# Turned probabilities of an attention step: one copy of both heads in place of one copy per head

## What is computed

```python
# layer 0 (8 heads): compressed, selected and window attention, gated
o = gc[..., 0:1] * o_cmp + gc[..., 1:2] * o_slc + gc[..., 2:3] * o_win
# layer 1 (16 heads): attention over the keys an indexer picked
o = jnp.einsum('bgrqk,bqkgd->bqgrd', masked_softmax(s, mask), vg)
# layer 3 (16 heads): dilated attention, three patterns folded into one mask
o = dilated_attention(q, k, v)
```

## Time and profile before

| what | value |
|---|---|
| median of three runs | 2514.33 us |
| profiled execution, its own time | 2514.71 us |
| its span, first to last instruction | 2513.0 us |
| mean granted TensorE clock | 0.980 of full speed |
| busy share: TensorE, VectorE, ScalarE, GpSimd | 96%, 53%, 37%, 43% |
| pass 0, pass 1, pass 2 in the span | 188 to 284, 837 to 925, 2021 to 2095 us |

### The profile page before, as it was taken

The page is one execution under the profiler, slowest core; times in us unless marked ns, Lnnn a source line. Parts: engine busy times, 40 slices in busy tenths (PEclk is TensorE's granted clock), DMA queues, the critical chain, the costliest instruction groups (busy, mean ns, idle before and its releaser), DMA issues.

```text
span 2513.0 us, 35279 instructions
## 1 busy us (share of the span) xinstructions
PE 2407.1 (96%) x12149; PEld 1946.9 (77%) x12149; DVE 1334.2 (53%) x2348; ACT 937.8 (37%) x1523; POOL 1085.3 (43%) x513
## 2 busy tenths in 40 slices
PE   7997989999999799999999989999999999999998
PEld 6774678888876467888887768888888967888887
DVE  6778664443157855111127976545366555545445
ACT  3356433222233463322234444322246364432222
POOL 2335334444443343444444734444454454444443
PEclk9999989999999899999999999999999999999999
DMA  7540235554322102323332213323333211232322
GB/s 308 195 149 26 98 132 190 184 184 159 99 94 76 34 34 76 106 95 96 97 100 84 76 51 119 113 87 101 100 101 102 91 34 48 87 109 84 109 92 75
DMA packets 64341, 263.64 MB, mean 105 GB/s; under 512 B 7265, under 2 KB 7777, under 8 KB 57953
## 3 DMA queue, kind: packets, MB, share of 16 engines
q1 hardware_dynamic: 61056, 251.00, 29.9%
q10 hardware_dynamic: 3168, 11.08, 1.2%
HBM read 259.95 MB, written 2.10 MB: 104 GB/s over the span
## 4 chain that ended last, share of the span: by engine, by line
PE 57%; issue 22%; POOL 9%; DVE 5%; ACT 2%; DVEq 2%; POOLq 1%; DMA 1%; SPq 0%; ACTq 0%
PE bank L638 17%; PE bank L640 17%; PE bank L639 17%; POOL w_lo L582 9%; PE bank L823 2%; PE bank L813 1%; DVEq L1761 1%; PE bank L842 1%; DVE acc L1559 1%; ACT prob L1282 1%; POOLq L629 1%; DVE bank L2177 1%; DVE prob L1741 1%; PE bank L760 0%; PE bank L659 0%
## 5 line engine op out<-in xcount | busy, mean ns | idle before, releaser
L582 POOL TENSOR_TENSOR w_lo<-raw,w_hi 128x1024 fp32r<-128x1024 f32 x378 | 918.1, 2437 | 1263.4 <-ACT w_hi L1168 1262.0
L638 PE MATMUL bank<-h_hi,w_hi 128*128 128x512 f32 x1760 | 698.4, 397 | 15.1 <-DVE h_lo L1606 7.8
L639 PE MATMUL bank<-h_lo,w_hi 128*128 128x512 f32 x1760 | 691.0, 393 | 0.0
L640 PE MATMUL bank<-h_hi,w_lo 128*128 128x512 f32 x1760 | 690.8, 393 | 0.0
L1168 ACT ACTIVATE w_hi<-raw 128x1024 fp32r<-128x1024 f32 x378 | 392.6, 1051 | 472.9 <-PE bank L640 469.9
L638 PE MATMUL bank<-g_hi,w_hi 128*128 128x512 f32 x1072 | 418.5, 390 | 0.0
L640 PE MATMUL bank<-g_hi,w_lo 128*128 128x512 f32 x1072 | 417.2, 389 | 0.0
L639 PE MATMUL bank<-g_lo,w_hi 128*128 128x512 f32 x1072 | 417.1, 389 | 0.0
L638 PEld LDWEIGHTS bank<-h_hi,w_hi 128*128 128x128 f32 x1760 | 334.3, 190 | 92.8 <-DVE h_lo L1606 8.7
L640 PEld LDWEIGHTS bank<-h_hi,w_lo 128*128 128x128 f32 x1760 | 334.1, 190 | 71.5
L639 PEld LDWEIGHTS bank<-h_lo,w_hi 128*128 128x128 f32 x1760 | 334.5, 190 | 68.5 <-issue 0.5
(11 more groups left out here) (298 smaller groups left out, 2610.5 us busy)
## 6 DMA issues: line engine op xcount, KB each, us to landing
raw<-in_panels SPq DMA_DIRECT2D x378, 512.0 KB, 3.5
modraw<-in_pairs SPq DMA_DIRECT2D x40, 1024.0 KB, 5.9
first_mods<-in_first SPq DMA_DIRECT2D x4, 2048.0 KB, 22.0
w<-in_w ACTq DMA_DIRECT2D x2, 2048.0 KB, 8.6
x<-in_x SPq DMA_DIRECT2D x1, 2048.0 KB, 8.3
out<-yout ACTq DMA_DIRECT2D x8, 256.0 KB, 2.2
mask<-in_causal ACTq DMA_DIRECT2D x1, 1024.0 KB, 5.7
mask<-in_dilated ACTq DMA_DIRECT2D x1, 1024.0 KB, 7.1
```

The lines of the kernel that those rows point to most:

```text
L582: pool.tensor_tensor(w_lo[:, slot, :], raw[:, slot, :], w_hi[:, slot, :].bitcast(F32), ALU.subtract)\
L638: pe.matmul(out, w_h, m_h, start=start, stop=False)
L639: pe.matmul(out, w_h, m_l, start=False, stop=False)
L640: return pe.matmul(out, w_l, m_h, start=False, stop=stop)
```

## The change

Banks 2 and 3 become one PSUM tensor, and one operation copies the same columns of both banks. ScalarE and VectorE do this by turns of steps. In pass 0 ScalarE has the even (wide) steps and VectorE the odd ones. In pass 1 ScalarE has all of the first 16 steps. In the rest of pass 1 and in pass 2 ScalarE has the steps with n mod 4 of 0 or 3, VectorE those with 1 or 2. `turn(n)` signals once, after both heads, and starts when both heads of step n-1 are copied.

```diff
-        bank = [ctx.enter_context(nc.psum_tensor(f"bank{n}", [P, 512], F32)) for n in range(8)]
+        bank = [None if n in (2, 3) else ctx.enter_context(nc.psum_tensor(f"bank{n}", [P, 512], F32)) for n in range(8)]
+        turned = ctx.enter_context(nc.psum_tensor("turned", [P, 2, 512], F32))
+        bank[2], bank[3] = turned[:, 0, :], turned[:, 1, :]
...
-        def odd_by_scalar(run, n):
-            return run == 0 and n % 2 == 1 or run == 1 and n < N_PAIR // 2 and n % 2 == 0
+        def copied_by_scalar(run, n):
+            return n % 2 == 0 if run == 0 else n % 4 in (0, 3) or run == 1 and n < N_PAIR // 2
...
                 def turn(n):
                     pe.wait_ge(weights_ready, at + n + 1)
-                    for b, copied in enumerate((pt_even, pt_odd)):
-                        if n:
-                            pe.wait_ge(copied, at + n)
+                    if n:
+                        pe.wait_ge(pt_copied, at + n)
+                    for b in range(2):
                         for j in range(pairs_[n][0] + 1):
                             m = pe.transpose(bank[2 + b][:, P * j:P * j + P],
                                              prob[:, PROB_SLOT[n % PROB_STEPS], b, P * j:P * j + P], ident[:, :])
-                        m.then_inc(pt_done, 1)
+                    m.then_inc(pt_done, 1)
...
-                    pe.wait_ge(pt_even, at + n + 1)
-                    pe.wait_ge(pt_odd, at + n + 1)
+                    pe.wait_ge(pt_copied, at + n + 1)
...
-                def copy_even(n):
-                    act.wait_ge(pt_done, 2 * (at + n) + 1)
+                def copy_turned(n):
+                    act.wait_ge(pt_done, at + n + 1)
                     if n >= 2:
                         act.wait_ge(pv_done, at + n - 1)
                     w = P * (pairs_[n][0] + 1)
-                    act.activation(probT[:, 2 * (n % 2), 0:w], bank[2][:, 0:w], ACT.Copy).then_inc(pt_even, 1)
-                    if odd_by_scalar(run, n):
-                        act.wait_ge(pt_done, 2 * (at + n) + 2)
-                        act.activation(probT[:, 2 * (n % 2) + 1, 0:w], bank[3][:, 0:w], ACT.Copy).then_inc(pt_odd, 1)
+                    act.activation(probT[:, 2 * (n % 2):2 * (n % 2) + 2, 0:w], turned[:, :, 0:w], ACT.Copy).then_inc(pt_copied, 1)
...
-                    if n >= SCORES_AHEAD:
-                        copy_even(n - SCORES_AHEAD)
+                    if n >= SCORES_AHEAD and copied_by_scalar(run, n - SCORES_AHEAD):
+                        copy_turned(n - SCORES_AHEAD)
...
-                def copy_odd(n):
-                    dve.wait_ge(pt_done, 2 * (at + n) + 2)
+                def copy_turned(n):
+                    dve.wait_ge(pt_done, at + n + 1)
                     if n >= 2:
                         dve.wait_ge(pv_done, at + n - 1)
                     w = P * (pairs_[n][0] + 1)
-                    dve.tensor_copy(probT[:, 2 * (n % 2) + 1, 0:w], bank[3][:, 0:w]).then_inc(pt_odd, 1)
+                    dve.tensor_copy(probT[:, 2 * (n % 2):2 * (n % 2) + 2, 0:w], turned[:, :, 0:w]).then_inc(pt_copied, 1)
...
-                    if n >= SCORES_AHEAD and not odd_by_scalar(run, n - SCORES_AHEAD):
-                        copy_odd(n - SCORES_AHEAD)
+                    if n >= SCORES_AHEAD and not copied_by_scalar(run, n - SCORES_AHEAD):
+                        copy_turned(n - SCORES_AHEAD)
```

More of the change, by code:

```diff
@@ L320, in build @@
         pt_done = sem("pt_done")
-        pt_even = sem("pt_even")
-        pt_odd = sem("pt_odd")
+        pt_copied = sem("pt_copied")
         pv_done = sem("pv_done")
@@ L1288, in attention @@
                 for n in range(N_PAIR - SCORES_AHEAD, N_PAIR):
-                    copy_even(n)
+                    if copied_by_scalar(run, n):
+                        copy_turned(n)
                     if group_ended(run, n - 1):
@@ L1739, in masked @@
                     if n >= PROB_STEPS:
-                        dve.wait_ge(pt_done, 2 * (at + n - PROB_STEPS) + 2)
+                        dve.wait_ge(pt_done, at + n - PROB_STEPS + 1)
                     dve.tensor_tensor_reduce(row_of(n, b, w), bank[SBANK[(2 * n + b) % 3]][:, 0:w], mask[:, i, 0:w],
@@ L1790, in attention @@
                 for n in range(N_PAIR - SCORES_AHEAD, N_PAIR):
-                    if not odd_by_scalar(run, n):
-                        copy_odd(n)
+                    if not copied_by_scalar(run, n):
+                        copy_turned(n)
                     if group_ended(run, n - 1):
```

## The result

The changed kernel takes 2521.17 us, the median of 6 runs (2519.45 to 2528.27); the kernel before, run beside it, 2514.1 (6 runs, 2512.0 to 2514.89). The ratio is 1.0033, 95% interval 1.002 to 1.0046: slower by 7.1 us. A second measurement of the same two kernels gave 2520.84 (7 runs) against 2513.95 (10 runs), ratio 1.003, 1.0019 to 1.0042. The profiled execution after took 2519.45 with a span of 2517.7; before it was 2514.71 and 2513.0.

A forecast was written before the change was run, and what follows sets the result against it. The prediction took chains of waits through the copy, not full engines, to bound the attention passes. Terms +6.4, +3.1 and -1.4 sum to +8.1 on 2514.71, giving 2522.8, less 0.4 for the median: 2522.4 us, range 2517 to 2526.

The forecast's parts named there:

- the mechanism in pass 2: Pass 2: exps, `out_high`, `out_low` and next masking stand behind the copy; rounds of 4.36 become 4.90 and 4.72 us.
- the end of pass 0: Pass 0, last steps draining one by one, with VectorE copying step 31: +0.45 us.
- Pass 2: Pass 2: even rounds +0.54 or +0.41, odd +0.36 or +0.23, end 1.2; together +6.4 us.
- The price of the copy: Joined copy of 2 x 512 columns, start to next start: 0.90 us on ScalarE, 1.14 on VectorE.
- Pass 1: Pass 1: rounds 9 to 14 and the end as in pass 2, rounds 1 to 8 put at 0; +3.1 us.
- Pass 0: Pass 0: VectorE loses the wide copy, gains the narrow one and reaches the inversion sooner in most rounds; -1.4 us.
- A late pass is passed on in full.: Behind each pass: TensorE begins a projection at once, so the passes' +8.1 us reaches the whole time.
- The wait before `out_low`: Pass 2, VectorE's wait for `out_high`, 0.75 us before: claimed to grow in even rounds.
- The second: Whole kernel: engine time decides, long copies are made up next round; about -4 us, 2510; chance 0.16.
- The third: Copy over two banks costs two single ones: +1.7 us, 2524; chance 0.12 together with the fourth.
- The fourth: Pass 0 gains nothing, ScalarE's wide copy (0.90 us) delaying exps and `out_high`: 2524; chance 0.12 together with the third.
- The rule: Skill's grouping advice: larger operations help saturated engines, smaller pieces where others wait; passes 1 and 2 put under the latter.

The follow-up runs named there:

- e1: Kernel before, with only the change's joined signal and wait, copies still split per head; 2517.5 us (one run).
- e3: Changed kernel; VectorE has every joined copy in pass 1's second half and pass 2, ScalarE the last ones of pass 0; 2522.0 us (one run).
- e2: Changed kernel, with every joined copy on ScalarE; 2512.8 us (one run).
- e7: Changed kernel, with VectorE's copies placed behind the masking of the second head and the inversion; 2523.6 us (one run).
- e8: Changed kernel once more, unedited; 2520.84 us (7 runs).
- e9: Kernel before once more, unedited; 2513.95 us (10 runs).
- e4: Kernel before, with one joined copy per step by ScalarE in all of pass 0; 2505.06 us (8 runs), ratio 0.9966.
- e10: Kernel before, with ScalarE also copying the second head of pass 0's wide steps, in two operations a step; 2500.91 us (4 runs), ratio 0.9944.
- e11: Kernel before, copies split: ScalarE copies both heads in pass 0, VectorE's copies stand behind second-head masking and inversion; 2499.49 us (5 runs), ratio 0.9944.

## Why the prediction came out right, point by point

The direction and the time held (2522.4 forecast, 2521.2 measured), and so did the mechanism in pass 2, which e1 to e3 show. The time held partly by luck: the passes grew by 11.9 us and not by 8.1, and the rest of the program, put at 0, became shorter. Three terms were mis-sized or left out: the end of pass 0, the start of ScalarE's copy in the first half of pass 1, and the clock outside the passes.

- **Pass 2, +6.4 forecast, +6.5 measured** (+6.6 in the second pair). Even rounds +0.53 (0.54 forecast) and +0.44 (0.41); odd +0.36 (0.36) and +0.25 (0.23); the end behind round 15 +1.22 (1.2): the 20 last matmuls of the earlier trace rows begin 8.02 after the start of round 15 (at 2099.09) where it was 6.71. Rounds 0 to 2, put at 0 but for round 2's 0.54, gave 0.53 together. e1 excludes the wait, e2 and e3 show each term alone.
- **The price of the copy.** 1.02 and 1.22 us for 2 x 512, start to next start 0.92 and 1.14, where 0.90 and 1.14 were put. The Trainium skill, "VectorE: DVE Perf Modes", section "The TRN2 errata — SBUF-src ops pay a fixed extra latency per instruction", gives 172 + N cycles at 1.2 GHz for a ScalarE copy out of PSUM and 120 + N at 0.96 for VectorE; for N = 1024 that is an estimate of 1.00 and 1.19 us. The trace agrees within 3%.
- **Pass 1, +3.1 forecast, +3.9 measured** (+4.0 in the second pair). Rounds 9 to 14 and the end gave 2.06 + 1.22, near the forecast 1.9 + 1.2. The first half was put at nothing, since ScalarE's joined copy of a wide step would begin 0.05 later than the first of its two had. That is the step that failed. The first of the two needed one turned head only; the joined one needs both, and begins 0.4 us later. Round 8, first before (it begins at 886.42), then after (885.87):

```profile
887.79 1.09 PE L823 MATMUL bank<-ident,prob 128*128 128x128 f32 x8
...
888.48 0.60 ACT L1256 ACTIVATE probT<-bank 128x512 f32<-128x512 f32 x1
```

```profile
887.24 1.09 PE L824 MATMUL turned<-ident,prob 128*128 128x128 f32 x8
...
888.37 1.02 ACT L1256 ACTIVATE probT<-turned 128x1024 f32<-128x1024 f32 x1 [0.60 <-PE turned L824]
```

Both turns begin 1.37 after the round's start, the copy 0.69 and 1.13 after the turn's, and the round takes 5.14 for 4.77. Rounds 2 and 4 together grew by 0.67 (0.75 in the second pair); in round 4 TensorE turns at the lower clock, 1.97 us for 1.09, and the copy begins 1.15 and 2.01 after the turn's start. Rounds 6 and 7 became 0.2 shorter each. e1, with the joined signal and the copies still split, has at least the same growth (round 8 5.21, rounds 2 and 4 together 15.06 for 14.13), so here it is the signal that costs and not the copy.
- **Pass 0, -1.4 forecast, +1.4 measured** (+0.6 in the second pair, where round 2 of the kernel before was longer). Here is the term that was mis-sized most. The rounds gave -1.44 against -1.85: round 2 -1.41 (-1.35), round 4 -0.27, round 12 -0.36 (-0.35), and round 3 went the other way, +0.32 for -0.27. The end gave +2.8 in place of +0.45, which had left out that the copy of step 29 stands behind VectorE's side work. Its timeline after:

```profile
278.13 0.55 DVE L1845 SCALAR_TENSOR_TENSOR modsum<-modraw,csil,modsum 128x256 f32<-128x256 f32 x1
278.60 0.15 DVE L1755 RECIPROCAL stat<-stat 128x2 f32<-128x2 f32 x1
...
278.93 0.69 DVE L1749 COPY probT<-turned 128x512 f32<-128x512 f32 x1
...
279.76 0.84 PE L824 MATMUL turned<-ident,prob 128*128 128x128 f32 x6 [2.19 <-DVE probT L1749]
...
281.60 1.09 PE L824 MATMUL turned<-ident,prob 128*128 128x128 f32 x4 [0.33 <-ACT probT L1256]
282.62 2.17 PE L842 MATMUL bank<-probT,vtok 128*64 128x128 f32 x20
```

Step 29's turn was done by 276.4, but its copy stands on VectorE behind `h_lo`, the side work and two operations for the weights, and the turn of 30 waits 2.19 us for it. Counted from the start of round 15 (272.50 here, 274.53 before) that turn comes 7.26 us later, against 5.81: +1.45. Then TensorE's clock falls (at 281.0 by the clock records), which the windows show, first after, up to and behind 281.6:

```profile
275.00:281.60 6.60, 3.61 (x40) 2.42 (x35) 3.61 (x12) 2.74 (x7) 3.07 (x3) 0.95 0.26 88
281.60:285.00 3.40, 3.40 (x25) 2.90 (x26) 0.69 (x1) 0.16 (x1) 0.00 (x0) 0.59 0.36 142
```

then the last of pass 0 before:

```profile
280.60:284.00 3.40, 3.15 (x39) 2.38 (x37) 0.76 (x3) 1.15 (x3) 1.04 (x1) 1.00 0.61 217
```

The turn of 31 takes 1.09 us where it took 0.66, the last 20 matmuls 2.17 where 1.35: another +1.25; the remaining 0.13 lies between the starts of the turns of 30 and 31. With ScalarE copying steps 29 and 31 (e3) the wait is 0.87, for GpSimd, no such stretch follows, and the end costs +0.33 only. So VectorE's late copy is shown as the cause of the wait; that the wait brings the lower clock goes with the profiles (both of the changed kernel and e7 have such an end, none of the other ten), but no run changed the clock alone.
- **"A late pass is passed on in full."** This failed. The passes grew by 11.9 us (11.2 in the second pair), the spans by 4.7 and 5.4, for the rest is 7.1 and 5.8 us shorter. What I took as untouched code at a fixed price depends on how the clock stands in it (see e8 and e9). The 3.8 us by which the passes were under-priced are more than made up by this. The profiled execution after was also the shortest of its six, 1.7 us below their median, and the one before lay 0.6 above its own, so the medians differ by 7.1 again. That the sum came out within 1.2 us of the median is luck.
- **The wait before `out_low`.** I had it grow in even rounds. It grows in odd ones (0.75 to 1.94, row at 2057.46), where VectorE has no wide copy between its maskings and `g_lo`; in even rounds it stays at 0.75. In pass 2 it goes from 13.1 us in 16 waits to 21.8 in 15.
- **Rivals.** The second (engine time decides) fell: a busy sum smaller by 4.4 us in pass 2 shortened nothing, and the rounds grew. The third (no saving over two banks) fell by the 0.92 and 1.14. The fourth (pass 0 gains nothing) came true in its number and not by its mechanism: in e2 and e4 ScalarE has all the copies of pass 0, the wide ones with them, and the pass is at 90.7 and 91.0, 5 to 6 us below the kernel before.
- **The rule.** The Trainium skill, "Perfetto Trace Analysis", section "Optimizing Scalar/DVE Operations", has grouping help a saturated engine, and smaller pieces help where others wait. The runs agree in sign: in pass 2 the changed kernel against e1 (+0.25 to +0.53 a round), though there the joined copy also moves a whole step to one engine and a part is order on VectorE, and in pass 0 e4 against e10, with the same engine, 0.6 us.

## What to carry to other kernels

Before joining two operations that ran side by side on two engines, look for what stands behind each in its engine's order: here the fixed cost saved was 0.04 to 0.06 us, and each steady round of pass 2 became 0.25 to 0.53 us longer. A joined copy also can't begin before both of its parts are there: 0.4 us a round where one engine had done both heads. The same trace then says what does help, namely to give the copy to the engine that has nothing urgent behind it, and to issue it behind the small operation that another engine waits for. The passes became 5.5 us shorter by the first (e10) and 9.5 by both (e11), each of 260.5; the 14 us of the whole in either case hold also what the clock gave back elsewhere. Price a pass's last steps by themselves, since there a copy stands behind side work that in the steady rounds is harmless.

## What the runs showed of the hardware

TensorE's granted clock falls to its lower level (1.2 GHz) for single stretches of this kernel, and which stretches these are repeats for one kernel and differs between versions. Summed over the span it is at the lower level for 101.4 and 100.3 us in the two profiles before, for 86.3 and 86.8 after. The two profiles of one kernel agree in the rest of the program within 0.9 us, while kernels whose code there is the same differ by up to 8.1 (2252.5 before, 2244.4 in e10). So a difference of a few microseconds between two versions of a pass can be lost or doubled elsewhere: e11's passes are 4.0 us shorter than e10's, its time 1.4. One stretch stands right behind a wait: TensorE idled 2.19 us before the turn of step 30, the clock fell 1.2 us after that turn's start, and over the 3.4 us from the turn of 31 it was 0.59. A second fact: a VectorE or ScalarE copy of 2 x 512 columns out of two PSUM banks in one operation ran at 1.22 and 1.02 us, 0.04 to 0.06 below two single ones from start to next start.
